# Forty background slices moved from the delta rule's scan into the block inversions

## The chip, the core and the metric

The kernel runs on one core of a Trainium2 chip. The metric is the device time of one execution, in microseconds (us); lower is better. TensorE is called PE here (PEld: its weight loads), VectorE DVE, ScalarE ACT, GpSimd POOL, and SP is the engine that issues the DMAs.

## What is computed

Three transformer blocks follow one another on a sequence of 512 tokens of width 1024. The change is in the third, whose core is a gated delta rule with 8 heads of 128, worked in chunks of 64 tokens. Beside it stand the gates of the block: a SiLU gate on the delta rule's output and a sigmoid that weighs it in the mix. Both are products of the block's input `h` with weights and have nothing to do with the recurrence.

```python
def _chunk_gated_delta_rule(q, k, v, beta, g):
    ...
    decay = jnp.exp(jnp.where(incl, gc[..., :, None] - gc[..., None, :], -jnp.inf))
    kb = k * beta[..., None]
    m = jnp.where(strict, jnp.einsum('bnhid,bnhjd->bnhij', kb, k) * decay, 0.0)
    a = m + jnp.eye(CHUNK, dtype=m.dtype)
    ...
    sol = lax.linalg.triangular_solve(a, rhs, left_side=True, lower=True, unit_diagonal=True)
    ...
    def step(state, inp):
        qg_n, kg_n, u_n, w_n, attn_n, gl_n = inp
        v_new = u_n - jnp.einsum('bhcd,bhde->bhce', w_n, state)
        o = jnp.einsum('bhcd,bhde->bhce', qg_n, state) + jnp.einsum('bhij,bhje->bhie', attn_n, v_new)
        state = state * jnp.exp(gl_n)[..., None, None] + jnp.einsum('bhcd,bhce->bhde', kg_n, v_new)
        return state, o
...
    o = o * o_norm_w.astype(jnp.float32) * jax.nn.silu(z.astype(jnp.float32).reshape(shp))
...
        mixed = jax.nn.sigmoid(gate_a) * y_a + jax.nn.sigmoid(gate_b) * y_b
```

## The kernel before

`deltanet` does the delta rule in stages, each a block of the program that ends with all engines meeting: the rows of the gates' scalars (`gate_rows`), the normalisation of q and k (`norm_tiles`), transposes, then four rounds `c` of two heads each, and at last the scan over the eight chunks. A round has two stages. `delta_matrices` makes the two heads' triangular matrices: PE blocks at L3022, L3027 and L3033, ACT's exponentials at L3045 and L3049, a chain of three POOL operations (L3004, L3007, L3010), DVE products at L3061 to L3068. `invert` inverts them by doubling, in five levels `l`. A level is a PE block at L926 (16 matmuls), a copy of its result by ACT (L951), a PE block at L938 and L939 (32 matmuls), and DVE additions (L969, L970) that the next level reads. POOL masks the matrices (L908).

`delta_scan` goes through eight chunks in order. A chunk has five PE blocks of 8 matmuls: state times key (L3102), the solved rows (L3108), the state's update (L3114), and two for the output (L3123, L3125). DVE works between the first and the second (L3147, L3150), between the second and the third (L3156), and adds to the state (L3162); POOL decays the state (L3139). All of these are in f32, where the profile has two records for each matmul. The five blocks do not have one shape. L3102 uses all 128 rows of the array and has 128 columns moving; L3108 and L3114 use 64 rows with 128 columns; L3123 uses 128 rows with 64 columns; L3125 uses 64 rows with 64 columns.

Into these stages `Background` puts the 16 output tiles of the two gates, 8 slices each, 128 in all. A slice is three matmuls of 128 rows and 512 columns (L171 to L173, inputs and weights split into a high and a low part). A stage names its gaps, the places in PE's program between its own blocks, and how many slices go to each; the slices are dealt out in order. In `invert` a level has two gaps, the first between L926 and L938, the second behind L939. In the scan the three gaps of a chunk are behind L3102, behind L3108 and behind L3125.

When the eighth slice of a tile is done, three further things follow on the other engines, in the gap in which it ended. ACT makes the high part of a later chunk of weights (L144) and applies SiLU (L3191, tiles 0 to 7) or sigmoid (L3193, tiles 8 to 15) to the result. DVE makes the low part (L149) and for the tiles from 8 on multiplies into the gate (L3198). SP issues the next load of weights. They stand in each engine's program before or behind the stage's own work:

```python
    def act(self, act, gap):
        for i in self.ended(gap):
            next_hi(self.k, act, self.g0 + i)
            self.evac_act(act, i, self)
```

`gate_rows` takes 8 slices, `norm_tiles` 16, the four `delta_matrices` 24 (two in each of three gaps), the four `invert` 40 (one in each of ten gaps), and the scan 40 (three, two and none in the gaps of a chunk). The first block's inversions use the same function with other fillers and are not touched.

Of the kernel before, what the change touches and what calls it, by code (L numbers as in the profile page):

```python
# [71 lines left out]
@contextmanager  # L72
def stage(nc, *names):


    first = SEM_SETS[_uses[0] % 2]
    _uses[0] += 1
    with ExitStack() as ctx:
        sems = [ctx.enter_context(nc.semaphore(n, first + i)) for i, n in enumerate(names)]
        with nc.Block() as block:  # L80
            yield (block, *sems)
        nc.gpsimd.sem_clear(range(first, first + len(names)))
# [34 lines left out]
def col(k, name, i=0):  # L117
    c = VEC[name] + i
    return k.vecs[:, c:c + 1]
# [11 lines left out]
def bcast_last(ap, n):  # L131

    return ap.rearrange("p (m a) -> p m a", a=1).broadcast_to([ap.shape[0], ap.shape[1], n])
# [105 lines left out]
def dense(k, n_out, kt, h, evac_act, evac_dve, sems=(), banks=4, pool=None, credits=()):  # L239


    hi, lo = h
    per = (kt + 7) // 8
    unroll = 4 * per
    tiles = unroll // per

    def entries(b):
        c, f = b % per, b // per
        return (1 if c == 0 else 0), [
            (k.ps[:, f % banks, :], hi[:, t, :], lo[:, t, :], (t - 8 * c) * P, P, t == 0, t == kt - 1, False)  # L250
            for t in range(8 * c, min(kt, 8 * c + 8))]

    def wrap(evac):
        def at(eng, j, b, S):
            if b % per == per - 1:
                fl = b // per
                evac(eng, j * tiles + fl, j * (tiles // 2) + fl // 2, fl % banks, S)
        return at
    linear(k, n_out * per, unroll, entries, wrap(evac_act), wrap(evac_dve), banks, sems, pool,
           credits)  # L260
# [79 lines left out]
def copy_out(k, dst):  # L340

    def act_evac(act, f, half, bank, S):
        act.activation(tile_at(dst, f), k.ps[:, bank, :], ACT.Copy).then_inc(S.acc_free, 1)
    return act_evac
# [629 lines left out]
def transpose_tiles(k, pairs):  # L974

    with stage(k.nc, "turned", "copied") as (block, turned, copied):
        jobs = [(src, dst, T) for src, dst in pairs for T in range(TT)]

        @block.tensor
        def _(pe):  # L980
            for n, (src, dst, T) in enumerate(jobs):
                if n >= 4:
                    pe.wait_ge(copied, n - 3)
                for c in range(4):
                    mm = pe.transpose(k.ps[:, n % 4, c * P:(c + 1) * P],
                                      src[:, c, T * P:(T + 1) * P], mat(k, "ident"))
                mm.then_inc(turned, 1)

        @block.scalar
        def _(act):  # L990
            for n, (src, dst, T) in enumerate(jobs):
                act.wait_ge(turned, n + 1)
                act.activation(dst[:, T, :], k.ps[:, n % 4, :], ACT.Copy).then_inc(copied, 1)
# [2183 lines left out]
def deltanet(k, qkv, h, gate, mix_d):  # L3177

    nc = k.nc
    q, key, v = qkv[:, 0:8, :], qkv[:, 8:16, :], qkv[:, 16:24, :]  # L3180
    with ExitStack() as ctx:
        sb = lambda n, s: ctx.enter_context(nc.sbuf_tensor(k.name(n), s, F32))
        beta, nbeta, g, egc, ekg = (sb(n, [P, TT, 8]) for n in ("beta", "nbeta", "g", "egc", "ekg"))
        egl = sb("egl", [P, 8, 8])
        mix_saved = ctx.enter_context(nc.semaphore("mix_saved", 106))

        def act_evac(act, i, bg):
            if i == 0:
                act.wait_ge(mix_saved, 16)
            if i < 8:  # L3190
                act.activation(gate[:, i, :], bg.bank(i), ACT.Silu).then_inc(bg.left, 1)  # L3191
            else:
                act.activation(bg.bank(i), bg.bank(i), ACT.Sigmoid).then_inc(bg.passed, 1)  # L3193

        def dve_evac(dve, i, bg):
            if i >= 8:
                dve.wait_ge(bg.passed, i - 7)
                dve.tensor_tensor(gate[:, i - 8, :], gate[:, i - 8, :], bg.bank(i), ALU.mult).then_inc(bg.left, 1)  # L3198

        with nc.sbuf_tensor(k.name("ba"), [P, 1, SEQ], F32) as ba:  # L3200
            dense(k, 1, DT, h, copy_out(k, ba), nothing)
            bg = Background(k, ctx, 16, h, (6, 7), act_evac, dve_evac)
            with stage(nc, "sent") as (block, sent):
                @block.sync
                def _(sp):
                    sp.dma_start(mix_d, gate[:, :, :]).then_inc(mix_saved, 16)
            gate_rows(k, ba, beta, nbeta, g, egc, ekg, egl, bg, 8)
        norm_tiles(k, [qkv[:, t, :] for t in range(16)], lambda n: (P ** -0.5 if n < 8 else 1.0), 1.0, 1e-6,
                   bg=bg, slices=4)
        k_tok, v_tok = sb("k_tok", [P, TT, D]), sb("v_tok", [P, TT, D])  # L3210
        transpose_tiles(k, [(src[:, 4 * i:4 * i + 4, :], dst[:, :, 512 * i:512 * i + 512])
                            for src, dst in ((key, k_tok), (v, v_tok)) for i in range(2)])
        with stage(nc, "scaled") as (block, scaled):
            @block.vector
            def _(dve):
                for T in range(TT):
                    kt = k_tok[:, T, :].rearrange("p (h n) -> p h n", n=P)
                    dve.tensor_tensor(kt, kt, bcast_last(ekg[:, T, :], P), ALU.mult).then_inc(scaled, 1)
        attn, xt = sb("attn", [P, 8, TT, 64]), sb("xt", [P, 8, TT, 64])
        at = [v[:, 0, 256 * n:256 * n + 256] for n in range(2)]  # L3220
        for c in range(4):
            delta_matrices(k, c, q, key, v[:, 2:8, :], nbeta, g, at, attn, bg, (2, 2, 2))
            invert(k, at, [xt[:, 2 * c + n, :, :].rearrange("p a n -> p (a n)") for n in range(2)], v[:, 2:8, :],
                   bg, (1, 1))
        delta_scan(k, q, key, k_tok, v_tok, xt, attn, beta, egc, egl, v, bg, (3, 2, 0))
        assert bg.at == 8 * bg.n
        nc.gpsimd.sem_clear(range(104, 107))
    norm_tiles(k, [v[:, t, :] for t in range(8)], lambda n: col(k, "o_norm"), 1.0 / P, 1e-6)
# [69 lines left out]
def third_block(k, x, h, pool_in, p_d):  # L3298
    nc = k.nc
    gain = lambda name: (lambda t: col(k, name, t))  # L3300
    with ExitStack() as outer:
# [3 lines left out]
        with nc.sbuf_tensor("qkv3", [P, 24, SEQ], F32) as qkv:  # L3305
            qkv_projection(k, h, qkv)
            mix_d = nc.dram_tensor("mix_saved_d", (P, DT, SEQ), F32, kind="Internal").ap()
            deltanet(k, qkv, h, x, mix_d)
            o = qkv[:, 16:24, :]
            with nc.sbuf_tensor("o3_hi", [P, DT, SEQ], F32R) as oh, \  # L3310
                    nc.sbuf_tensor("o3_lo", [P, DT, SEQ], F32R) as ol:
                merge(k, o, x, mix_d, (oh, ol))
                dense(k, DT, DT, (oh, ol), nothing, residual(k, h, x), ("first",))
# [268 lines left out]
```

## Time and profile before

| | |
|---|---|
| median of 3 runs | 3761.19 us (3743.45 to 3762.63) |
| the profiled execution | 3744.08 us, of which the span of the trace is 3742.1 us |
| granted TensorE clock, mean | 0.93 of full speed |
| PE busy | 3339.5 us, 89% |
| PEld busy | 2592.6 us, 69% |
| DVE busy | 1754.9 us, 47% |
| ACT busy | 1201.4 us, 32% |
| POOL busy | 145.0 us, 4% |
| rounds c = 0 to 3 (matrices and inversions) | 2783 to 2990 us |
| the scan's eight chunks | 2990 to 3106 us |

The busy time of PE is the time in which at least one matmul is under way, each counted from its issue to its modelled end; an issue follows the one before sooner than that end. So how long work takes PE is read from starts, not from durations. The granted clock is the share of full speed that the chip let the array run at; 1.00 is 2.4 GHz and 0.50 is 1.2 GHz.

### The profile page before, as it was taken

To read this page: it belongs to the slowest core of one execution; us is meant where nothing else is said; L and a number is where in the kernel's file an instruction comes from. 1 tells how busy PE (TensorE), PEld (TensorE's weight loads), DVE (VectorE), ACT (ScalarE), POOL (GpSimd) and SP (SyncE) were. 2 spreads that over 40 slices of the span, in tenths; PEclk is the share of its full clock that TensorE was granted. 3 is DMA by queue.
4 is the path that set the end of the run, shared out by engine and by line. 5 is a ranking of instruction groups with operands and counts; after the bars stand their busy time and mean duration, and the time that the engine had idled before them with its cause. 6 is when DMAs were issued, how large, how long until landed. Compare 5 with 4: busy or idle time off the path is not lost. (4 is left out here: it accounts for less than half of the span.)

```text
span 3742.1 us, 43214 instructions
## 1 busy us (share of the span) xinstructions
PE 3339.5 (89%) x17816; PEld 2592.6 (69%) x17816; DVE 1754.9 (47%) x2659; ACT 1201.4 (32%) x1732; POOL 145.0 (4%) x174
## 2 busy tenths in 40 slices
PE   8999988886899989999999999969778796799986
PEld 6888766674688868774477888657656684577764
DVE  4447547533444456766654333345523344433323
ACT  3332332224433333232343222233362213332322
POOL 0000001210000000000000000000014310000000
PEclk9999998778999999998999999989879898899998
DMA  3335220000233543320022333212300001122221
GB/s 131 101 118 205 94 71 24 2 7 1 98 99 97 179 152 113 96 68 6 1 90 79 97 100 97 79 53 88 97 17 24 24 23 51 51 86 89 90 83 69
DMA packets 75219, 285.23 MB, mean 76 GB/s; under 512 B 8336, under 2 KB 8464, under 8 KB 73872
## 3 DMA queue, kind: packets, MB, share of 16 engines
q1 hardware_dynamic: 75024, 282.47, 23.3%
q8 instruction: 142, 2.33, 0.3%
q14 instruction: 53, 0.43, 0.0%
HBM read 276.15 MB, written 6.29 MB: 75 GB/s over the span
## 5 line engine op out<-in xcount | busy, mean ns | idle before, releaser
L149 DVE TENSOR_TENSOR wlo<-raw,whi 128x1024 fp32r<-128x1024 f32 x450 | 552.2, 1227 | 1299.8 <-ACT whi L144 1299.5
L144 ACT ACTIVATE whi<-raw 128x1024 fp32r<-128x1024 f32 x450 | 476.2, 1059 | 1250.6 <-PE ps L173 823.2
L171 PE MATMUL ps<-h_hi,wlo 128*128 128x512 f32 x1216 | 492.0, 405 | 49.9 <-PEq L80 21.2
L173 PE MATMUL ps<-h_hi,whi 128*128 128x512 f32 x1216 | 478.9, 394 | 0.0
L172 PE MATMUL ps<-h_lo,whi 128*128 128x512 f32 x1216 | 478.8, 394 | 0.0
L171 PEld LDWEIGHTS ps<-h_hi,wlo 128*128 128x128 f32 x1216 | 231.3, 190 | 114.1 <-issue 51.1
L233 PE MATMUL ps<-h_hi,wlo 128*128 128x512 f32 x584 | 233.5, 400 | 59.7 <-DVEq L204 59.7
L173 PEld LDWEIGHTS ps<-h_hi,whi 128*128 128x128 f32 x1216 | 231.3, 190 | 49.3
L172 PEld LDWEIGHTS ps<-h_lo,whi 128*128 128x128 f32 x1216 | 232.1, 191 | 47.1 <-issue 2.2
L234 PE MATMUL ps<-h_lo,whi 128*128 128x512 f32 x584 | 232.0, 397 | 0.0
L235 PE MATMUL ps<-h_hi,whi 128*128 128x512 f32 x584 | 231.5, 396 | 0.0
L171 PE MATMUL ps<-mid_hi,wlo 128*128 128x512 f32 x528 | 207.8, 394 | 0.0
L173 PE MATMUL ps<-mid_hi,whi 128*128 128x512 f32 x528 | 205.4, 389 | 0.0
L172 PE MATMUL ps<-mid_lo,whi 128*128 128x512 f32 x528 | 205.4, 389 | 0.0
L1794 DVE SCALAR_TENSOR_TENSOR conv_acc<-u,vecs,conv_acc 128x512 f32<-128x512 f32 x232 | 174.0, 750 | 5.8
L233 PEld LDWEIGHTS ps<-h_hi,wlo 128*128 128x128 f32 x584 | 112.8, 193 | 86.1 <-issue 62.5
L171 PE MATMUL ps<-hx_hi,wlo 128*128 128x512 f32 x304 | 121.9, 401 | 11.1 <-PEq L104 6.5
L235 PEld LDWEIGHTS ps<-h_hi,whi 128*128 128x128 f32 x584 | 112.6, 193 | 24.1
L234 PEld LDWEIGHTS ps<-h_lo,whi 128*128 128x128 f32 x584 | 112.9, 193 | 23.6
L172 PE MATMUL ps<-hx_lo,whi 128*128 128x512 f32 x304 | 120.0, 395 | 0.0
L173 PE MATMUL ps<-hx_hi,whi 128*128 128x512 f32 x304 | 119.6, 393 | 0.0
L171 PEld LDWEIGHTS ps<-mid_hi,wlo 128*128 128x128 f32 x528 | 99.1, 188 | 21.9 <-issue 1.4
(582 smaller groups left out, 5690.6 us busy)
## 6 DMA issues: line engine op xcount, KB each, us to landing
raw<-in_wstream SPq DMA_DIRECT2D x453, 512.0 KB, 3.5
mod_ring<-in_wmod SPq DMA_DIRECT2D x48, 512.0 KB, 4.5
c_rows<-in_c_rows SPq DMA_DIRECT2D x3, 1024.0 KB, 5.6
x<-in_x_t SPq DMA_DIRECT2D x4, 512.0 KB, 8.5
x_saved<-x SPq DMA_DIRECT2D x1, 2048.0 KB, 9.0
x<-x_saved SPq DMA_DIRECT2D x1, 2048.0 KB, 9.2
mix_saved_d<-x SPq DMA_DIRECT2D x1, 2048.0 KB, 8.6
mix_back<-mix_saved_d SPq DMA_DIRECT2D x1, 2048.0 KB, 7.8
```

The lines of the kernel that those rows point to most:

```text
L144: act.activation(k.whi[:, n % SPLIT, :], k.raw[:, n % RAW, :], ACT.Copy).then_inc(k.hi_ready, 1)
L149: dve.tensor_tensor(k.wlo[:, n % SPLIT, :], k.raw[:, n % RAW, :], k.whi[:, n % SPLIT, :].bitcast(F32), ALU.subtract).then_inc(k.split_read ...
L171: pe.matmul(out, wlo, hi, start=first, stop=False)
L172: pe.matmul(out, whi, lo, start=False, stop=False)
L173: return pe.matmul(out, whi, hi, start=False, stop=last)
L233: pe.matmul(out, lo, xhi, start=first, stop=False)
L234: pe.matmul(out, hi, xlo, start=False, stop=False)
L235: mm = pe.matmul(out, hi, xhi, start=False, stop=last)
L1794: dve.scalar_tensor_tensor(out, row[:, tap:tap + SEQ], w, acc[:, :], ALU.mult, ALU.add)\
```

## The change

Two tuples in `deltanet`. `invert` gets two slices in each of its gaps where it had one (4 rounds of 10 gaps, so 80 slices for 40), and the scan gets none (0 for 40). The number of slices, their order and everything that they compute stay as they were. Since the slices are dealt out in order, the gaps in which a tile ends move too.

```diff
@@ -3221,8 +3221,8 @@
         for c in range(4):
             delta_matrices(k, c, q, key, v[:, 2:8, :], nbeta, g, at, attn, bg, (2, 2, 2))
             invert(k, at, [xt[:, 2 * c + n, :, :].rearrange("p a n -> p (a n)") for n in range(2)], v[:, 2:8, :],
-                   bg, (1, 1))
-        delta_scan(k, q, key, k_tok, v_tok, xt, attn, beta, egc, egl, v, bg, (3, 2, 0))
+                   bg, (2, 2))
+        delta_scan(k, q, key, k_tok, v_tok, xt, attn, beta, egc, egl, v, bg, (0, 0, 0))
```

PE at the first gap of the first inversion, before (qkv, xt and mats are the inversion's own operands, h the block's input, whi and wlo the weights):

```order
L926 MATMUL ps<-qkv 64x64 x16
L171 MATMUL ps<-h_hi_16109,wlo 128x512
L172 MATMUL ps<-h_lo_16110,whi 128x512
L173 MATMUL ps<-h_hi_16109,whi 128x512
L938 MATMUL ps<-qkv,xt 64x64
```

The piece of the difference at the same place shows that the second slice stands directly behind the first, ahead of L938:

```order
+L171 MATMUL ps<-h_hi_16109,wlo 128x512
+L172 MATMUL ps<-h_lo_16110,whi 128x512
+L173 MATMUL ps<-h_hi_16109,whi 128x512
+L938 MATMUL ps<-qkv,xt 64x64
+L939 MATMUL ps<-xt,qkv 64x64
```

PE in the scan from one L3108 to the next chunk, now:

```order
L3102 MATMUL ps<-state,qkv 64x128 x8
L3108 MATMUL ps<-r_158,xt 64x128 x8
L3114 MATMUL ps<-r_158,k_tok 128x128 x8
L3123 MATMUL ps<-qkv,state 128x64 x8
L3125 MATMUL ps<-attn,r_158 128x64 x8
```

Before, nine rows of L171 to L173 stood between the first and the second of these, and six between the second and the third.

ACT in `delta_matrices` of the round c = 2, now:

```order
L3045 ACT_TABLE_LOAD
L3045 ACTIVATE qkv<-ps 128x512
L3049 ACTIVATE qkv<-ps 128x512
L144 ACTIVATE whi<-raw 128x1024
L3193 ACT_TABLE_LOAD
L3193 ACTIVATE ps<-ps 128x512
L3045 ACT_TABLE_LOAD
L3045 ACTIVATE qkv<-ps 128x512
L3049 ACTIVATE qkv<-ps 128x512
```

Before, no tile ended in this stage, and the four exponentials stood behind one table load. Now a tile ends in the stage's third gap at c = 1, its second at c = 2 and its first at c = 3.

## Rows read from the trace of the kernel before

**Rows 1.** Busy time by stretch: the first inversion, the scan.

```profile
core 0: us, PE busy (x) PEld busy (x) DVE busy (x) ACT busy (x) POOL busy (x), PEclk, DMA share, GB/s
2802.00:2835.00 33.00, 27.56 (x510) 21.95 (x510) 10.32 (x22) 8.11 (x15) 10.22 (x14) 0.90 0.06 18
...
2990.00:3106.00 116.00, 111.62 (x760) 96.37 (x760) 48.30 (x42) 12.50 (x18) 15.87 (x9) 0.97 0.08 27
```

**Rows 2.** PE's timeline, one inversion level (start, us, engine, line, operands, [idle before]).

```profile
2818.31 1.15 PE L926 MATMUL ps<-qkv 64*64 64x64 f32 x32
...
2819.72 0.39 PE L172 MATMUL ps<-h_lo,whi 128*128 128x512 f32 x1
2819.95 0.40 PE L173 MATMUL ps<-h_hi,whi 128*128 128x512 f32 x1
2820.28 0.34 PE L938 MATMUL ps<-qkv,xt 64*64 64x64 f32 x4
...
2823.24 1.15 PE L926 MATMUL ps<-qkv 64*64 64x64 f32 x32
```

**Rows 3.** Groups by line of the four rounds: what L938 waited for.

```profile
L938 PE MATMUL ps<-qkv,xt 64*64 64x64 f32 x512 | 33.9, 229 | 5.4 <-ACT qkv L951 5.4
```

**Rows 4.** Timeline of ACT where a tile ends in the first inversion.

```profile
2812.06 1.06 ACT L144 ACTIVATE whi<-raw 128x1024 fp32r<-128x1024 f32 x1 [4.61 <-PE ps L173]
2813.13 1.28 ACT L3191 ACT_TABLE_LOAD   x1
2814.43 0.60 ACT L3191 ACTIVATE x<-ps 128x512 f32<-128x512 f32 x1
```

**Rows 5.** Timeline where the first inversion ends and the next round begins.

```profile
2831.78 0.40 PE L173 MATMUL ps<-h_hi,whi 128*128 128x512 f32 x1
...
2833.30 1.23 DVE L149 TENSOR_TENSOR wlo<-raw,whi 128x1024 fp32r<-128x1024 f32 x1 [1.55 <-ACT whi L144]
...
2835.47 0.47 PE L171 MATMUL ps<-h_hi,wlo 128*128 128x512 f32 x1 [3.30 <-PEq L80]
```

**Rows 6.** Timeline of PE: slices at the low clock.

```profile
2784.18 0.63 PE L173 MATMUL ps<-h_hi,whi 128*128 128x512 f32 x1
2784.61 0.63 PE L171 MATMUL ps<-h_hi,wlo 128*128 128x512 f32 x1
```

**Rows 7.** Timeline of PE and DVE in the scan's third chunk.

```profile
3020.58 1.96 PE L3102 MATMUL ps<-state,qkv 128*64 128x128 f32 x16
...
3023.83 1.22 DVE L3150 TENSOR_TENSOR r<-v_tok,r 64x1024 f32<-64x1024 f32 x1
...
3025.10 1.96 PE L3108 MATMUL ps<-r,xt 64*64 64x128 f32 x16 [0.29 <-DVE r L3150]
...
3027.10 1.22 DVE L3156 TENSOR_TENSOR r<-ps,beta 64x1024 f32<-64x1024 f32 x1 [2.05 <-PE ps L3108]
...
3028.57 2.05 PE L3114 MATMUL ps<-r,k_tok 64*128 64x128 f32 x16
```

**Rows 8.** Timeline of PE: the scan's second and fifth chunk begin.

```profile
3006.13 1.96 PE L3102 MATMUL ps<-state,qkv 128*64 128x128 f32 x16
...
3048.25 3.41 PE L3102 MATMUL ps<-state,qkv 128*64 128x128 f32 x16
```

**Rows 9.** Busy time and clock: around the two low stretches of the scan.

```profile
2990.75:2994.10 3.35, 3.35 (x16) 3.26 (x16) 0.00 (x0) 0.00 (x0) 1.90 (x1) 0.52 0.31 124
...
3045.00:3048.30 3.30, 3.30 (x30) 3.17 (x29) 0.73 (x1) 0.00 (x0) 0.00 (x0) 1.00 0.02 5
3048.30:3051.60 3.30, 3.30 (x18) 2.97 (x17) 0.00 (x0) 0.60 (x1) 1.90 (x1) 0.54 0.00 0
```

**Rows 10.** Busy time and clock: two stretches of the first block.

```profile
752.00:788.00 36.00, 30.58 (x125) 21.99 (x125) 16.79 (x70) 8.07 (x30) 1.71 (x3) 0.54 0.00 1
...
822.00:878.00 56.00, 54.43 (x719) 48.51 (x719) 23.20 (x50) 4.74 (x8) 0.00 (x0) 0.99 0.01 2
```

**Rows 11.** Groups by line of 752 to 788: the costliest on PE.

```profile
L1315 PE MATMUL ps<-a_t,rw 64*128 64x128 f32 x16 | 5.6, 447 | 2.0 <-PEq L80 2.0
```

## The prediction

> **What bounds the kernel here.** I read four views. The busy time by stretch says who has room: in an inversion PE has a matmul under way for 27.6 of 33 us, in the scan for 111.6 of 116 us, at a mean clock of 0.97, while DVE is at 48 of 116 us [rows 1]. That would make the scan look full of PE work. The timeline corrects it. In the third chunk L3102 starts at 3020.58 and takes PE about 1.9 us; the DVE operation on which L3108 waits ends at 3023.83 + 1.22 = 3025.05, and L3108 starts at 3025.10. L3156 ends at 3028.32, and L3114 starts at 3028.57 [rows 7]. So both gaps with slices are bounded by DVE, not by PE, or nearly so: the slices fill waits that stay when they go. In an inversion it is the other way round. From one L926 to the next there are 4.93 us, L938 follows the last slice at its own pace, and no row of that level has an idle time before it [rows 2]: PE is the bound, and what is added there is paid. The third view is the granted clock, which fell twice in the scan and stood low for long stretches of the first block [rows 9, 10]. The fourth is the groups by line, for the waits inside the inversions [rows 3].
>
> **The change part by part, against the profiled execution of 3744.1 us.**
>
> *Slices in the inversions.* Four rounds of ten gaps get one slice more, 40 slices. Matmuls of a slice start 0.23 us apart (2819.72 to 2819.95 [rows 2]), three make 0.69 us: 40 x 0.69 = +27.6 us. The first gap of each round comes when the clock is low; there matmuls start 0.43 us apart [rows 6], 0.6 us more for a slice, four times: +2.4. What is hidden: L938 waited 5.4 us in all for ACT's copy, because a tile ended in the gap ahead [rows 3]. That gap no longer ends a tile in three rounds and is longer in all: -5.4. The work behind a tile's end on ACT is 1.06 + 1.28 + 0.60 = 2.9 us where a table has to be loaded [rows 4], and the copy of 0.4 us comes behind it, 3.4 in all. Ahead of the next L938 PE has now 1.1 us of L926 and 1.6 of slices. Of the tile ends in a second gap two have a table load (c = 1 and c = 3): +0.7 each, +1.5. The others are covered, in a first gap by L938 and L939 (some 2 of the level's 4.93 us) too, and DVE's part likewise. Together +26.1.
>
> *Where tiles end.* Every inversion ended a tile in its last gap. Behind PE's last matmul (to 2832.18) came L144 and then L149 to 2834.53, and the next round's PE work started at 2835.47 [rows 5]: 2.35 us in which the round could not end. At c = 1 and 2 no tile ends in the last two gaps (-2.35 each), at c = 0 one ends in the last but one (-1.7), c = 3 stays: -6.4. A shorter wait there may also save some of the low clock at a round's start (a slice there costs 0.6 us more [rows 6]); I take -2, with -5 and 0 as ends. In exchange three tiles end in the matrices. At c = 1 the new L149 stands behind DVE's last product: its own 1.23 us [rows 5]. At c = 2 the exponential waits for 1.06 + 1.28 + 0.60 and a second load of 1.28, 4.2 us [rows 4]. The four matmuls of L3022 ahead of it take 1.0 us by the pace of L3102's eight [rows 7] and wait for POOL besides, so the delay is between 0 and 3.2; I take +1.9. At c = 3 it is 2.9 us, between 0 and 1.9; I take +1.5. POOL's chain queues behind that exponential, and the matrices wait for POOL. Sum +4.6. SP's loads are issued as early as before relative to the tiles; tiles end 12 us apart at the least, and the DMA engines are 6% busy [rows 1]. Nothing there. Together -3.8.
>
> What the Trainium skill adds on tables (ScalarE: Activation LUTs, What ACT_TABLE_LOAD costs): a switch costs a load of 1.28 us and a drain of 1.38 besides. The row has the same 1.28, but the ACTIVATE starts 0.02 us after the load's end [rows 4]; with the drain the sum would be about 5 us higher.
>
> *Slices out of the scan, the clock held.* Two chunks took 3048.25 - 3020.58 = 27.67 us [rows 7, 8], 13.84 each. Without slices L3114 comes 0.05 us after L3156, as L3108 does after L3150, and not 0.25: -0.2, and a little for the change of operands, -0.26 x 8 = -2.1. One chunk took 3020.58 - 3006.13 = 14.45 [rows 7, 8], since L149 and L3198 stood ahead of L3156: -0.6, and -0.3 for the others. Together -3.0. So the 27.6 us of slices that leave the scan give back 3.
>
> *The clock in the scan.* This is the term that decides. At 3045 to 3048.3 PE had no idle time, only the blocks L3123 and L3125, with 64 columns moving; right behind it the clock was 0.54, and L3102 took 3.41 us for 1.96 [rows 8, 9]. So narrow work can cost the clock without any wait. It happened once in 110 us because slices and L3102, full-height and wide, stood in nearly every other stretch. Now L3102 is the only such block in a chunk of 13.6 us; behind it come a DVE wait of 2.6 us, the half-height L3108, a wait of 1.4, the half-height L3114, and the two narrow blocks. I expect the clock to fall in every chunk. What brings it back? At 2990.75, after an idle stretch, the scan began at 0.52, and one L3102 later it was up [rows 9]. But from 752 to 788 it stood at 0.54 with PE busy for 30.6 of 36 us, mostly half-height matmuls such as L1315 [rows 10, 11]; the first block's own scan, at 0.99 [rows 10], has extra full-height matmuls of no use to the result in its waits. So only L3102 lifts the clock here, and what follows it is the 2.6 us wait, where a fast clock is worth nothing. Price: a low L3102 costs 1.45 us more [rows 8]; the other four blocks have no row at the low clock, but each took 1.9 us in all and has as many records, so I take 1.5 for each of the five. Lower end 0 (the clock holds), upper end 5 x 1.5 x 8 = 60. I take 54, close to the upper end, because a low stretch lasts until the next L3102 ends, and only a little of L3108 falls into a high one.
>
> **Sum:** 26.1 - 3.8 - 3.0 + 54 = +73 us, with the scan at about 165 us instead of 116. Against the profiled execution this is 3817. The three timed runs and the profile are two near 3743 and two near 3762; I put the base between them, at 3753, and forecast **3826 us**, 1.7% over the median of 3761.
>
> **The rivals.**
>
> *The clock holds in the scan.* For it: the new waits, 2.6 and 1.4 us, are short, and PE is at work between them. Against it: a fall without any wait [rows 9] and a long low stretch with PE busy [rows 10, 11]. Then the sum is 26.1 - 3.8 - 3.0 = +19, a time of 3772. The Trainium skill speaks for this one (TensorE: Matmul & The Clock Gate, HAM oscillation): it has waits with an idle PE as what takes the clock down, long ones such as those for a DMA. By that rule a stream with short waits keeps its clock; the trace does not agree, since the clock fell behind 3.3 us of busy PE [rows 9].
>
> *The clock falls but half comes back.* If the half-height blocks hold it up once it is up, the cost is L3102 and one or two blocks of a chunk, 1.5 to 3 us, 12 to 24 in all: 3784 to 3796. Against it: half-height work did not bring the clock up in the first block's low stretch [rows 10, 11].
>
> *The second slices fall into idle time, and nothing gets slower.* An inversion has 33.0 - 27.6 = 5.4 us without a matmul [rows 1], four of them nearly 22, and the matrices have more. If this lay in the gaps, at 0.69 us or more in each of the 40, the 27.6 would be free, and the scan's -3.0 and the tiles' ends would stay: -6.8, with the clock held 3746. It decides only if both the gaps have room and the clock holds. Against it: a level without an idle row [rows 2]; the idle time is at the inversion's ends, where POOL and DVE start the round [rows 5].
>
> **Chances.** The forecast 0.78; half comes back 0.08; the clock holds 0.10; free slices 0.04. A measurement of this kernel can tell about 0.5% from no change, 19 us of 3761. The clock-holds case lies at +19 with a spread of some 10 us, so 0.05 of its 0.10 goes to slower. Slower 0.91, within 0.5% 0.08, faster 0.01. The range: the forecast's own is 3800 to 3850 (the clock term 40 to 60, the base 3743 to 3762, the tiles' ends a few us). To leave out no more than two in ten it reaches down over most of the case with half: 3785 to 3850.
>
> **What would show it.** In the profile after: the scan's stretch at 155 to 170 us with a mean clock near 0.6 and L3102 to L3125 at 3.4 us in most chunks; L3150 to L3108 still 0.05 us apart; a steady inversion level at 6.3 us for 4.93, rounds c = 0 to 3 some 20 us longer in all. Wrong would be: a scan of 113 us at a clock of 0.95 or above (the clock step fails), or inversion levels still near 5 us (PE was not the bound there).

## The result and the profile after

The changed kernel takes 3833.15 us (median of 4 runs, 3822.05 to 3835.72) for 3758.02 us before (4 runs): a ratio of 1.0196, 95% interval 1.0164 to 1.0229. That is 75 us more; the profiled executions have spans of 3831.8 and 3742.1 us.

I cut both traces at the same instructions: the first slice of the round c = 0, the first L3102, and the start of the last L3125.

| stretch | before, us | after, us | difference |
|---|---|---|---|
| up to the rounds | 2783.2 | 2794.2 | +11.0 |
| the four rounds | 207.5 | 226.1 | +18.6 |
| the scan | 114.1 | 172.4 | +58.3 |
| from there on | 637.0 | 638.8 | +1.8 |

The first line is time in code that the change does not touch; it comes back in the last section. The second and third make 76.9 us, close to the 75 us between the medians.

Busy time by stretch of the kernel after: the first chunk and the whole scan. The columns are those of [rows 1].

```profile
3020.50:3042.60 22.10, 18.23 (x81) 16.97 (x81) 4.87 (x4) 0.07 (x1) 1.72 (x1) 0.50 0.03 12
...
3020.50:3193.70 173.20, 141.60 (x640) 131.64 (x639) 39.08 (x32) 4.69 (x8) 14.99 (x8) 0.55 0.01 2
```

PE does 640 matmul records where it did 760, ACT and DVE have less to do, and the stretch is half as long again. The column that goes with it is the granted clock, 0.55 for 0.97 [rows 1]. DVE's operations take what they took, 1.22 or 1.23 us each. The timeline of PE and DVE over the second chunk shows both:

```profile
3042.43 3.64 PE L3102 MATMUL ps<-state,qkv 128*64 128x128 f32 x16
...
3047.36 1.22 DVE L3150 TENSOR_TENSOR r<-v_tok,r 64x1024 f32<-64x1024 f32 x1
3048.64 3.07 PE L3108 MATMUL ps<-r,xt 64*64 64x128 f32 x16 [2.58 <-DVE r L3150]
3051.74 1.23 DVE L3156 TENSOR_TENSOR r<-ps,beta 64x1024 f32<-64x1024 f32 x1 [3.16 <-PE ps L3108]
3053.03 3.77 PE L3114 MATMUL ps<-r,k_tok 64*128 64x128 f32 x16 [1.32 <-DVE r L3156]
3056.73 3.67 PE L3123 MATMUL ps<-qkv,state 128*128 128x64 f32 x16
...
3060.34 3.67 PE L3125 MATMUL ps<-attn,r 64*128 64x64 f32 x16
```

L3108 starts 0.06 us behind L3150 (3047.36 + 1.22 = 3048.58) and L3114 0.06 us behind L3156, so PE's idle waits of 2.6 and 1.3 us, which it did not have before, are waits for the same DVE operations, which the slices used to cover [rows 7]. All five blocks are slow: 3.64, 3.07, 3.77, 3.67 and 3.67 us, where the high clock has 1.96 to 2.05 for L3102, L3108 and L3114 [rows 7]. L3108 alone was partly at the high clock.

In the inversions the timeline of PE has, for one level:

```profile
2830.70 1.15 PE L926 MATMUL ps<-qkv 64*64 64x64 f32 x32
...
2832.12 0.39 PE L172 MATMUL ps<-h_lo,whi 128*128 128x512 f32 x1
2832.35 0.40 PE L173 MATMUL ps<-h_hi,whi 128*128 128x512 f32 x1
2832.58 0.39 PE L171 MATMUL ps<-h_hi,wlo 128*128 128x512 f32 x1
...
2837.01 1.09 PE L926 MATMUL ps<-qkv 64*64 64x64 f32 x30
```

A level takes 6.31 us for 4.93 [rows 2]: 1.38 us, two slices of 0.69, and still no idle time. What L938 waited for, in the groups by line over the four rounds, has nearly gone, 0.7 us for 5.4 [rows 3]:

```profile
L938 PE MATMUL ps<-qkv,xt 64*64 64x64 f32 x512 | 32.7, 224 | 0.7 <-ACT qkv L951 0.7
```

### The profile page after: what moved, and what is told of

Its sections match the earlier page's. It is cut to its first block and busy times, and to the rows that moved or that the text cites. A ratio compares the mean times of both kernels' runs of the same rounds, so it can differ in the third digit from the quotient of the medians.

```text
span 3831.8 us, 43216 instructions
## 1 busy us (share of the span) xinstructions
PE 3409.2 (89%) x17816; PEld 2659.3 (69%) x17816; DVE 1751.9 (46%) x2659; ACT 1205.5 (31%) x1734; POOL 144.4 (4%) x174
## 5 line engine op out<-in xcount | busy, mean ns | idle before, releaser
L171 PE MATMUL ps<-h_hi,wlo 128*128 128x512 f32 x1216 | 490.2, 403 | 39.6 <-DVE wlo L149 12.0
L173 PE MATMUL ps<-h_hi,whi 128*128 128x512 f32 x1216 | 478.6, 394 | 0.0
L171 PEld LDWEIGHTS ps<-h_hi,wlo 128*128 128x128 f32 x1216 | 231.6, 190 | 101.8 <-issue 45.4
L173 PEld LDWEIGHTS ps<-h_hi,whi 128*128 128x128 f32 x1216 | 231.3, 190 | 49.3
L171 PE MATMUL ps<-mid_hi,wlo 128*128 128x512 f32 x528 | 207.8, 394 | 0.0
L173 PE MATMUL ps<-mid_hi,whi 128*128 128x512 f32 x528 | 205.4, 389 | 0.0
L1794 DVE SCALAR_TENSOR_TENSOR conv_acc<-u,vecs,conv_acc 128x512 f32<-128x512 f32 x232 | 174.0, 750 | 5.8
L171 PE MATMUL ps<-hx_hi,wlo 128*128 128x512 f32 x304 | 121.9, 401 | 11.1 <-PEq L104 6.5
L173 PE MATMUL ps<-hx_hi,whi 128*128 128x512 f32 x304 | 119.6, 393 | 0.0
L172 PEld LDWEIGHTS ps<-mid_lo,whi 128*128 128x128 f32 x528 | 99.1, 188 | 21.9 <-issue 1.4
```

Of the source, the lines that this page charges most:

```text
L171: pe.matmul(out, wlo, hi, start=first, stop=False)
L172: pe.matmul(out, whi, lo, start=False, stop=False)
L173: return pe.matmul(out, whi, hi, start=False, stop=last)
L1794: dve.scalar_tensor_tensor(out, row[:, tap:tap + SEQ], w, acc[:, :], ALU.mult, ALU.add)\
```

## The experiments

Two questions: is it the clock that makes the scan longer, and what holds the clock up? And what did the 80 slices cost in the inversions? Every scan below goes from the start of the first L3102 to the start of the last L3125 record. The first two experiments, the fewer fillers and the nine in one wait start from the changed kernel. Half of the change, the scan's part alone and the two versions at the end are shown against the kernel before. The added lines move the scan's blocks: in the kernels with fillers L3102 has become L3106, and L3125 L3131; the text goes on calling them by their old lines.

**Full-height matmuls in the waits.** Each extra matmul multiplies two constant matrices into a part of TensorE's output memory that the scan does not use.

```diff
+        def fill(pe, n):
+            for _ in range(n):
+                pe.matmul(k.ps[:, 7, 0:P], mat(k, "ident")[0:128, :], mat(k, "ones")[0:128, :], start=True, stop=True)
...
                 bg.pe(pe, gaps[3 * j])
+                fill(pe, 6)
                 pe.wait_ge(r0_ready, j + 1)
...
                 bg.pe(pe, gaps[3 * j + 1])
+                fill(pe, 3)
                 pe.wait_ge(vn_ready, j + 1)
```

> The changed kernel, and in the scan's two waits PE gets matmuls of no use to the result: six behind L3102 and three behind L3108, each of 128 rows and 128 columns, some 0.2 us each, so 1.3 and 0.6 us in waits of 2.6 and 1.4 us. Theory (the scan pays for the clock): the clock stays up in nearly all of the scan, which goes from 172.4 to 111-118 us, and the whole kernel comes out some 57 us under the changed one, at 3770 to 3780. Rival (the scan got longer for another reason than the clock, or more matmuls only add work): scan 172 us or more, kernel 3830 or more.

Measured: 3770.47 us (10 runs, ratio to before 1.0027, interval 1.0014 to 1.004), and a scan of 112.2 us, the shortest of the first six. The rounds stayed at 226.1. Busy time of the scan:

```profile
3009.00:3121.50 112.50, 101.28 (x784) 93.16 (x784) 39.09 (x32) 4.18 (x7) 15.21 (x9) 0.96 0.01 5
```

Work that is thrown away, 72 matmuls, took 60 us out of the scan. The rival falls: with the clock up, nothing of the longer scan is left. The two parts of the change are separated with it: with the clock held, the scan without slices is 1.9 us shorter than before, and what remains of the loss lies in the rounds: 18.6 - 1.9 = 16.7 us, beside 15.4 between the medians (3755.07 us for the kernel before, measured beside it).

**The same, at half height.** The edit is the same with `[0:64, :]` in both operands.

> The same as e1_wide, same count and same columns, but each of the extra matmuls uses only 64 rows of the array. PE is under way as long as in e1_wide. Theory (half-height work counts for less towards the clock): the clock is low for most of the scan, which takes 135 to 165 us; kernel 3795 to 3825. Rival (only PE's busy time counts): the same as e1_wide, scan 111-118 us, kernel 3770 to 3780.

Measured: 3833.3 us (ratio 1.0202, interval 1.018 to 1.0224), scan 174.0 us. Busy time of the scan:

```profile
3020.70:3195.00 174.30, 169.17 (x784) 158.79 (x784) 39.07 (x32) 4.18 (x7) 15.16 (x8) 0.55 0.01 3
```

PE has a matmul under way for 169.2 of 174.3 us, a greater share than in any other scan of this study, and the clock is as low as with the empty waits. The number of matmuls, their columns and their places are those of the kernel at 0.96. Only the rows of the array differ, and with them the work in each matmul. So PE's busy time does not tell what clock it will get, and the rival falls. I had expected these fillers to help some of the way, with a scan of 135 to 165 us; they gave nothing, and the scan is 1.6 us longer than with empty waits (172.4).

**Fewer full-height matmuls.** Four and two instead of six and three.

> As e1_wide, full-height extra matmuls, but only four behind L3102 and two behind L3108 (0.9 and 0.4 us of the waits of 2.6 and 1.4 us). Theory (full-height work holds the clock up, and too little of it doesn't): a mixed scan, low stretches in some chunks, 115 to 155 us, between e1_wide's 110 and the 172 of none. Rival (any full-height work in the waits is enough): scan 110-113 us.

Measured (one execution): 3793.35 us, scan 130.5 us at a mean clock of 0.80. As the theory had it: some chunks low, some high. The block durations in the trace show the first chunk's last two blocks, the third chunk from L3108 on, and the whole fourth at the low clock, the last three chunks at the high one.

```profile
3021.00:3151.80 130.80, 116.34 (x736) 106.73 (x736) 39.09 (x32) 4.20 (x8) 15.15 (x8) 0.80 0.01 3
```

**All nine in the first wait.** `fill(pe, 9)` behind L3102 and none behind L3108.

> As e1_wide, with the same nine full-height extra matmuls in a chunk, but all nine behind L3102 and none behind L3108, where the second wait and the half-height and narrow blocks then follow one another. Theory: the place counts, the clock falls behind L3108 to L3123 in most chunks and comes back with the next L3102; scan 135 to 155 us. Rival (the amount in a chunk is what counts): scan 110-118 us as in e1_wide.

Measured (one execution): 3801.53 us, scan 153.3 us.

```profile
3008.70:3162.40 153.70, 141.90 (x784) 132.78 (x784) 39.08 (x32) 4.18 (x7) 15.15 (x8) 0.68 0.01 3
```

The same work as in the first experiment, in another place, costs 41 us. In each of the eight chunks L3108 is fast and L3125 slow: the clock falls somewhere in L3114 or L3123 and is back after the next L3102. With nine of them, they have to stand in both waits; whether more in the first alone would do was not tried.

**Half of the change.**

```diff
-                   bg, (1, 1))
+                   bg, (2, 1))
-        delta_scan(k, q, key, k_tok, v_tok, xt, attn, beta, egc, egl, v, bg, (3, 2, 0))
+        delta_scan(k, q, key, k_tok, v_tok, xt, attn, beta, egc, egl, v, bg, (2, 1, 0))
```

> Half-way between the two kernels: two slices in the first and one in the second gap of an inversion level (60 in all), two and one in the scan's gaps (20, until they run out in the seventh chunk). Theory (clock): three slices in a chunk are enough to hold it up, the scan takes 111 to 122 us (the last chunk without slices may fall), the rounds 9 us more than before: kernel 3765 to 3780. Rival (each slice taken from the scan costs the same): half of the whole loss of 75 us, kernel near 3795.

Measured: 3767.09 us (9 runs, ratio 1.0033, interval 1.0021 to 1.0046), inside the theory's range and away from the rival's 3795. The parts came out otherwise than I had them, and the two misses, 7 us and more in the scan and 9 us in the rounds, cancelled. The scan took 129.0 us, above my 122: the clock fell in the first chunk at L3114, the second and third began with a low L3102, and it was low again from L3114 of the seventh chunk on, which has two slices and the eighth none. Chunks four to six ran at the high clock throughout. The rounds took 207.5 us, just what they took before, with 20 slices more. Their 13.8 us were paid for by where tiles end: with 15 slices in an inversion none of the four ends one in its last gap any more, though three end in the matrices. That puts the old places at about 14 us, net, and that includes whatever the longer gaps hide. For the changed kernel, where three inversions come free in this way, I had 5.4 + 6.4 + 2 - 4.6 = 9.

**The scan's part alone.**

```diff
-            bg = Background(k, ctx, 16, h, (6, 7), act_evac, dve_evac)
+            bg = Background(k, ctx, 11, h, (6, 7), act_evac, dve_evac)
...
-        delta_scan(k, q, key, k_tok, v_tok, xt, attn, beta, egc, egl, v, bg, (3, 2, 0))
+        delta_scan(k, q, key, k_tok, v_tok, xt, attn, beta, egc, egl, v, bg, (0, 0, 0))
```

> The kernel before with one slice in each gap of the inversions and none in the scan: the last five of the sixteen gate tiles are left out, and the weights of everything behind them are those of other tiles (the amount of that work is unchanged). Theory (clock in the scan): rounds 207 us as before, scan 170 to 175 us for 114, kernel 55 to 60 us above the one before, near 3815. Rival (the loss sits in the fuller inversions, and slices cost something in the scan): scan under 114 us, kernel 3750 to 3758.

Measured: 3812.71 us (4 runs, ratio 1.0154, interval 1.0131 to 1.0176), rounds 209.7 us, scan 174.2 us. Leaving out five sixteenths of the gates' products made the kernel 58 us slower (3755.07 us for the kernel before, measured beside it). The rival had the scan under 114 us.

**Two versions meant to beat both.** The scan's gaps are covered by slices for nothing, an inversion's are not. So the second question can be turned round: take the slices out of the inversions and put them where PE waits.

```diff
-            gate_rows(k, ba, beta, nbeta, g, egc, ekg, egl, bg, 8)
+            gate_rows(k, ba, beta, nbeta, g, egc, ekg, egl, bg, 16)
...
-                   bg=bg, slices=4)
+                   bg=bg, slices=7)
...
-            delta_matrices(k, c, q, key, v[:, 2:8, :], nbeta, g, at, attn, bg, (2, 2, 2))
+            delta_matrices(k, c, q, key, v[:, 2:8, :], nbeta, g, at, attn, bg, (2, 3, 6))
...
-                   bg, (1, 1))
+                   bg, (0, 0))
```

> A version meant to beat both: the scan keeps its 40 slices (three and two), the inversions get none, and the slices stand where PE waited in the trace of before: 16 in the gates' scalars (8 before), 28 in the normalisation (16), 44 in the matrices (24: two, three and six in a gap). Theory (a slice in an inversion is paid at 0.69 us or nearly, one in a wait of PE is free): the inversions lose up to 27 us, the tile ends in the normalisation and the matrices give back 10 to 15; kernel 10 to 20 us under the one before, 3735 to 3745. Rival (an inversion without slices waits for DVE and ACT instead, and the ends of tiles in the matrices delay POOL's chain): 3755 or more.

Measured: 3713.64 us (4 runs, 3713.15 to 3714.61), ratio 0.989, interval 0.9873 to 0.9907: 41 us under the kernel before and 120 under the changed one. The rounds take 167.3 us for 207.5, the scan 112.5, and the stages ahead with their 20 slices more are 0.6 us longer. A level of the inversion, timeline of PE:

```profile
2829.08 1.50 PE L926 MATMUL ps<-qkv 64*64 64x64 f32 x32
...
2832.25 1.50 PE L926 MATMUL ps<-qkv 64*64 64x64 f32 x32
```

3.17 us for 4.93 with a slice in each gap. A first slice in a gap costs 0.88 us then, and a second 0.69. Busy time of the rounds and the scan of this version:

```profile
2794.20:2961.50 167.30, 137.22 (x2311) 124.64 (x2311) 62.84 (x129) 49.56 (x80) 84.89 (x98) 0.90 0.07 21
2961.50:3075.00 113.50, 109.85 (x760) 94.53 (x758) 48.19 (x42) 12.59 (x19) 14.90 (x8) 0.98 0.08 24
```

The mean clock is 0.90 in the rounds and 0.98 in the scan. In the first inversion PE has no full-height matmul from 2812.5 to 2835.7 us, only L918, L926, L938 and L939, with 64 rows and 64 columns moving. Busy time and clock of two stretches of it:

```profile
2820.00:2823.00 3.00, 3.00 (x62) 3.00 (x60) 0.98 (x3) 0.00 (x0) 0.09 (x1) 0.50 0.02 5
2823.00:2834.80 11.80, 11.38 (x347) 10.78 (x344) 5.46 (x15) 3.07 (x8) 4.31 (x6) 0.99 0.02 4
```

So matmuls that are half-height and narrow, one by one, did bring the clock up and hold it here. In the kernel they stand in turn in the upper and the lower half of the rows, and 347 records in 11.8 us are one in 0.034 us, where the scan's blocks have one in 0.12 us (16 in 1.9 us [rows 7]). Which of the two matters was not tried apart. The gain was two to four times the forecast. By the levels it is 20 levels of 1.76 us, 35 us; the rest lies in the places of tile ends, less what they cost in the matrices, and was not taken apart.

The second version keeps one slice in a level's first gap:

```diff
-            gate_rows(k, ba, beta, nbeta, g, egc, ekg, egl, bg, 8)
+            gate_rows(k, ba, beta, nbeta, g, egc, ekg, egl, bg, 16)
...
-            delta_matrices(k, c, q, key, v[:, 2:8, :], nbeta, g, at, attn, bg, (2, 2, 2))
+            delta_matrices(k, c, q, key, v[:, 2:8, :], nbeta, g, at, attn, bg, (2, 3, 4))
...
-                   bg, (1, 1))
+                   bg, (1, 0))
```

> Between before and t1_bare: 16 slices in the gates' scalars, 16 in the normalisation as before, 36 in the matrices (two, three and four), 20 in the inversions (one in the first gap of a level, none in the second), 40 in the scan. Theory as for t1_bare: the inversions lose up to 14 us and the ends of tiles cost less; kernel 5 to 15 us under the one before, 3740 to 3750. Rival (the inversion's second gap was covered by DVE's additions, so nothing is gained): 3755 or more.

Measured: 3734.97 us (5 runs, ratio 0.9938, interval 0.9918 to 0.9958), rounds 187.0 us, scan 114.1. Half-way between the kernel before and the first version, as the levels would have it, and faster than the forecast's 3740 to 3750: the covered wait of the rival was not there.

## Why the prediction was right

- **PE bounds an inversion, DVE the scan's gaps.** Right on both counts: a level took 6.31 us where I had 6.3, and L3108 and L3114 start 0.06 us behind DVE's operations in the changed kernel.
- **The rounds**, forecast at 26.1 - 3.8 = +22, measured +18.6. One term can be read by itself: L938's wait fell by 4.7 us, where I had 5.4 less 1.5. The term that was mis-sized is that of the tile ends, -6.4 + 4.6 with the 2 us for the clock: the half-way version shows that the old places cost more than I gave them, about 14 us in all for my 9.
- **Slices out of the scan, clock held**, forecast at -3.0. The full-height fillers measure it: 112.2 for 114.1 us, -1.9 (both scans have two low L3102).
- **The clock in the scan**, forecast at +54 between 0 and 60, measured 172.4 - 112.2 = +60, at the upper end. The clock fell in every chunk, as forecast, and the size was 6 us short. I had 1.5 us for a block at the low clock, from L3102's durations, and a tenth of it back. L3102, L3114, L3123 and L3125 were slow in all eight chunks, at 1.7 us more each (3.67 and 3.77 for about 2.0); only L3108 had a share of the high clock, and cost 1.2 on average. Since the version with fillers has two low L3102 itself, that is 3 x 1.7 + 1.2 + 1.3 = 7.6 us for a chunk, 61 for eight, against the 60 measured.
- **The steps behind it.** That narrow or half-height work cannot hold the clock rested on one fall behind a busy PE [rows 9] and on the first block's low stretch [rows 10, 11]. The pair of experiments with the same matmuls at 128 and at 64 rows, clock 0.96 and 0.55, shows the height part directly for the scan's waits. The evidence that I gave for it was weaker than I wrote. The low stretch of [rows 11] has full-height matmuls too, L1334 and L1336, 11.0 of its 30.6 us, and those of L1336 have the form of L3102:

```profile
L1336 PE MATMUL ps<-rw,v_tok 128*64 128x128 f32 x16 | 5.5, 448 | 0.0
```

So that stretch does not show that half-height work is what kept the clock low, nor that a block such as L3102 lifts it. And the bare inversion at 0.99 is a case against the general form: 64-row matmuls with 64 columns can lift the clock and hold it. What held in the scan, that only its full-height work kept the clock, is shown for the scan's blocks at their pace. That narrow columns count for less, as I put it for L3123, was not tried alone.
- **The rivals.** The clock did not hold, nor did half of it come back; the slices did not fall into idle time. The page of the Trainium skill that I set against the forecast (TensorE: Matmul & The Clock Gate, HAM oscillation) names waits with an idle PE; the half-height experiment has hardly any such wait, 5 us in 174 and none longer than 1.0 us, and the low clock all the same.
- **The drain** that the Trainium skill adds to a table load (ScalarE: Activation LUTs, What ACT_TABLE_LOAD costs) would have made the rounds dearer than my sum; they were cheaper. That alone could be the other terms, but the trace has no such time: the ACTIVATE starts 0.02 us behind the load's end [rows 4].
- **The total** came out at +75 by the medians and +77 by the two stretches for a forecast of +73, because the clock's 6 us too few and the rounds' 4 too many partly cancelled. The agreement is better than the parts are, and that much of it is luck.

## What to carry to other kernels

Before you take filler work out of a stage because an engine looks full there, ask two things of each gap: what ends the wait if the filler goes, and what holds TensorE's clock then. Here 27.6 us of slices gave back 1.9 and cost 60, and nine useless full-height matmuls for each chunk in the same waits undid it. A busy share does not answer the second question: read the granted clock. And a filler is free only where TensorE waits anyway: the same forty slices cost 35 us in loops that had no idle time and next to nothing in stages that waited for POOL, DVE or ACT.

## What the runs showed that I had not expected

**Half-height fillers were worth nothing.** 72 matmuls that filled the waits as the full-height ones did left the clock at 0.55 and the scan at 174.0 us, where the full-height ones brought them to 0.96 and 112.2 us.

**The place of the fillers is worth 41 us** at the same amount: 153.3 us with nine in one wait, 112.2 with six and three.

**The same code of the first block took 92 or 104 us.** In the kernel before, the stretch up to 622 us ended 12 us earlier than in the kernel after, in code that the change does not touch. Busy time and clock, first before, then after:

```profile
530.00:622.00 92.00, 72.81 (x441) 55.35 (x439) 65.51 (x151) 23.51 (x54) 5.67 (x8) 0.89 0.15 46
```

```profile
530.00:634.00 104.00, 86.25 (x430) 65.80 (x430) 64.89 (x150) 21.86 (x51) 5.68 (x8) 0.72 0.13 41
```

DVE and ACT have nearly the same work, the clock is 0.72 for 0.89. Of the ten profiles, two kinds of start of the third block's gates came out, near 2710 us (before and three of the experiments) and near 2721 us (after and five), and the ten times of the first experiment fall into 3761 to 3762 and 3770 to 3773. The 18 times of the kernel before that were measured beside that experiment, 3744 to 3764, do not fall into two groups, so this is not all that varies. A single profile of this kernel can mislead by 11 us, and two are to be compared by stretches. What decides between the two was not looked into.
